# Moving the modulation's products from VectorE to GpSimd and their row sums to ScalarE in a 1-core, two-block transformer kernel

## The reference, cut to what matters

```python
c_act = jax.nn.silu(c)
for i in range(DEPTH_2):                       # 2 layers
    mod = (c_act @ ada_w[i] + ada_b[i])[:, None, :]    # 1024 x 6144 per layer
    sh_a, sc_a, g_a, sh_f, sc_f, g_f = jnp.split(mod, 6, axis=-1)
    h = rms_norm(x, norm_g[i, 0]) * (1.0 + sc_a) + sh_a
    y = attention(h, ...)
    x = x + g_a * rms_norm(y, norm_g[i, 1])
    h = rms_norm(x, norm_g[i, 2]) * (1.0 + sc_f) + sh_f
    x = x + g_f * rms_norm(swiglu_2(h, ffn_w_in[i], ffn_w_out[i]), norm_g[i, 3])
```

## Time and profile before

| | |
|---|---|
| median of 3 runs | 1020.12 us (1019.92 to 1020.59) |
| the profiled execution | 1019.76 us, its span 1018.3 us |
| PE | 992.9 us busy, 98% |
| PEld | 906.0 us, 89% |
| DVE | 687.5 us, 68% |
| ACT | 491.4 us, 48% |
| POOL | 32.1 us, 3% |
| mean DMA rate | 222 GB/s |

### The profile page before, as it was taken

The page is one execution under the profiler, slowest core; times in us unless marked ns, Lnnn a source line. Parts: engine busy times, 40 slices in busy tenths (PEclk is TensorE's granted clock), DMA queues, the critical chain, the costliest instruction groups (busy, mean ns, idle before and its releaser), DMA issues.

```text
span 1018.3 us, 15767 instructions
## 1 busy us (share of the span) xinstructions
PE 992.9 (98%) x6730; PEld 906.0 (89%) x6730; DVE 687.5 (68%) x986; ACT 491.4 (48%) x688; POOL 32.1 (3%) x51
## 2 busy tenths in 40 slices
PE   7999999899999999999999999999999899999997
PEld 6988899779898998899889999997997789999996
DVE  5766756769757767877768768667676766545443
ACT  5644544454334345555564343445667664434341
POOL 2000000010000000100000000001000010000000
PEclk9999999999999999999999999999999999999999
DMA  9653367646887875786467778875643257555511
GB/s 365 260 217 115 125 247 277 220 176 247 317 267 276 297 281 201 274 312 238 177 248 262 299 281 315 302 294 190 202 151 125 83 131 262 173 199 176 198 42 42
DMA packets 33302, 225.64 MB, mean 222 GB/s; under 512 B 3997, under 2 KB 4277, under 8 KB 6864
## 3 DMA queue, kind: packets, MB, share of 16 engines
q1 hardware_dynamic: 31104, 219.00, 59.8%
q0 software_dynamic: 1552, 4.88, 1.4%
q10 hardware_dynamic: 576, 0.74, 0.2%
HBM read 223.54 MB, written 1.08 MB: 221 GB/s over the span
## 4 chain that ended last, share of the span: by engine, by line
PE 88%; DVE 5%; ACT 3%; issue 1%; DMA 1%; POOL 0%; ACTq 0%; DVEq 0%
PE psum L569 18%; PE psum L571 18%; PE psum L570 18%; PE psum L595 8%; PE psum L596 8%; PE psum L597 8%; DVE low L496 2%; PE psum L815 2%; ACT high L490 1%; PE psum L660 1%; PE psum L661 1%; PE psum L662 1%; PE psum L311 1%; PE psum L881 1%; DMA x_res<-in_x 1%
## 5 line engine op out<-in xcount | busy, mean ns | idle before, releaser
L496 DVE TENSOR_TENSOR low<-raw,high 128x2048 fp32r<-128x2048 f32 (+1 forms) x160 | 362.0, 2275 | 162.0 <-ACT high L490 161.5
L569 PE MATMUL psum<-h_hi,high 128*128 128x256 f32 x1504 | 428.9, 285 | 0.0
L570 PE MATMUL psum<-h_lo,high 128*128 128x256 f32 x1504 | 425.5, 283 | 0.0
L571 PE MATMUL psum<-h_hi,low 128*128 128x256 f32 x1504 | 425.5, 283 | 0.0
L490 ACT ACTIVATE high<-raw 128x2048 fp32r<-128x2048 f32 (+1 forms) x160 | 300.8, 1898 | 50.0 <-DMA raw<-in_gate_up 28.9
L569 PEld LDWEIGHTS psum<-h_hi,high 128*128 128x128 f32 x1504 | 288.4, 192 | 4.9 <-issue 2.0
L570 PEld LDWEIGHTS psum<-h_lo,high 128*128 128x128 f32 x1504 | 288.5, 192 | 1.4 <-issue 0.2
L571 PEld LDWEIGHTS psum<-h_hi,low 128*128 128x128 f32 x1504 | 288.5, 192 | 0.0
L595 PE MATMUL psum<-high,y_hi 128*128 128x512 f32 x328 | 129.2, 394 | 2.2 <-DVE y_lo L903 1.7
L596 PE MATMUL psum<-low,y_hi 128*128 128x512 f32 x328 | 128.0, 390 | 0.0
L597 PE MATMUL psum<-high,y_lo 128*128 128x512 f32 x328 | 127.7, 389 | 0.0
(11 more groups left out here) (173 smaller groups left out, 848.2 us busy)
## 6 DMA issues: line engine op xcount, KB each, us to landing
raw<-in_gate_up SPq DMA_DIRECT2D x66, 1024.0 KB, 5.2
raw<-in_ada SPq DMA_DIRECT2D x48, 1024.0 KB, 5.7
raw<-in_down SPq DMA_DIRECT2D x33, 1024.0 KB, 5.2
raw<-in_mix SPq DMA_DIRECT2D x14, 1024.0 KB, 5.1
raw<-in_moba_qk SPq DMA_DIRECT2D x8, 1024.0 KB, 6.9
raw<-in_diff_qk SPq DMA_DIRECT2D x8, 1024.0 KB, 6.4
raw<-in_qk SPq DMA_DIRECT2D x4, 1024.0 KB, 15.8
raw<-in_branch SPq DMA_DIRECT2D x4, 1024.0 KB, 6.0
```

The lines of the kernel that those rows point to most:

```text
L496: nc.vector.tensor_tensor(low[i % N_RAW][:, s], raw[i % N_RAW][:, s], high[n % N_HI][:, s].bitcast(F32), ALU.subtract).then_inc(*rest.up(key))
L569: nc.tensor.matmul(to, a, hi(k), start=first, stop=False)
L570: nc.tensor.matmul(to, a, lo(k), start=False, stop=False)
L571: m = nc.tensor.matmul(to, r, hi(k), start=False, stop=last and j > j0)
```

## The change

The work of `dve_sum` is divided over three engines. GpSimd multiplies the two rows of an ada block by `c_row`, in place (`pool_weigh`, two instructions each, signal `weighed`); calls of it for runs of blocks stand between the other work in GpSimd's program. ScalarE sums each row by a Copy with an accumulator (`act_sum`), in its own order after the rounding of the first slab that stands three or more pieces later in the stream, and signals `summed`. VectorE only calls `dve_modulation` for a finished section, four or more pieces later.

```diff
+        POOL_AT = {m: i for i, (kind, m) in enumerate(STREAM) if kind == "ada"}
+
+        def pool_weigh(*blocks):
+            for m in blocks:
+                i = POOL_AT[m]
+                yield from pool.wait_ge(raw_in[i % N_RAW], i)
+                yield from pool.wait_ge(small_act, "c")
+                for a in range(2):
+                    w = raw[i % N_RAW][:, a * D:(a + 1) * D]
+                    nc.gpsimd.tensor_tensor(w, w, c_row[:, :], ALU.mult).then_inc(*weighed.up((m, a)))
...
-        def dve_sum(i, m):
-            raw_rows = raw[i % N_RAW][:, :].rearrange("p (a n) -> p a n", a=2)
-            yield from dve.wait_ge(raw_in[i % N_RAW], i)
-            yield from dve.wait_ge(small_act, "c")
+        def act_sum(i, m):
             for a in range(2):
-                w = raw_rows[:, a, :]
-                last = nc.vector.tensor_tensor_reduce(
-                    out=w, in0=w, in1=c_row[:, :], scale=1.0, scalar=0.0, op0=ALU.mult, op1=ALU.add,
-                    accum_out=mod_raw[:, 2 * m + a:2 * m + a + 1])
+                w = raw[i % N_RAW][:, a * D:(a + 1) * D]
+                yield from act.wait_ge(weighed, (m, a))
+                last = nc.scalar.activation(w, w, ACT.Copy, accum_out=mod_raw[:, 2 * m + a:2 * m + a + 1])
...
         def act_split(n):
             for i, kind, m in act.items(n):
-                if kind == "main":
-                    yield from act_round(i, m)
+                if kind == "ada":
+                    act_sums.append((i, m))
+                    continue
+                yield from act_round(i, m)
+                while act_sums and act_sums[0][0] + 3 <= i:
+                    yield from act_sum(*act_sums.pop(0))
 
         def dve_split(n):
             for i, kind, m in dve.items(n):
-                if kind == "main":
-                    yield from dve_rest(i, m)
-                else:
-                    yield from dve_sum(i, m)
+                if kind == "ada":
+                    dve_sums.append((i, m))
+                    continue
+                yield from dve_rest(i, m)
+                while dve_sums and dve_sums[0][0] + 4 <= i:
+                    yield from dve_section(dve_sums.pop(0)[1])
...
+            yield from pool_weigh(*range(8))
             yield from pool_post_norm(0)
             yield from pool_table()
+            yield from pool_weigh(*range(8, 12))
             yield from pool_spread()
+            yield from pool_weigh(*range(12, 16))
             yield from pool_gain(0, 0, None)
+            yield from pool_weigh(*range(16, 24))
             yield from pool_post_norm(1)
             yield from pool_gain(0, 1, 0)
+            yield from pool_weigh(*range(24, 32))
             yield from pool_post_norm(2)
+            yield from pool_weigh(*range(32, 48))
             yield from pool_post_norm(3)
```

More of the change, by code:

```diff
@@ L225, in build_program @@
         stored = sig("stored")
+        summed = sig("summed")
         rounded, squared, affined, evacuated, hi_made, exped, probs_copied, small_act = (sig(n) for n in (
             "rounded", "squared", "affined", "evacuated", "hi_made", "exped", "probs_copied", "small_act"))
-        rest, summed, modulated, joined, scaled, h_hi_made, h_lo_made, gained, x_made, produced, lo_made = (sig(n) for n in (
-            "rest", "summed", "modulated", "joined", "scaled", "h_hi_made", "h_lo_made", "gained", "x_made", "produced", "lo_made"))
+        rest, modulated, joined, scaled, h_hi_made, h_lo_made, gained, x_made, produced, lo_made = (sig(n) for n in (
+            "rest", "modulated", "joined", "scaled", "h_hi_made", "h_lo_made", "gained", "x_made", "produced", "lo_made"))
         squared_dve = sig("squared_dve")
@@ L236, in build_program @@
             "slab", "turned", "scored", "applied", "gathered", "small_pe"))
-        scaled_pool = sig("scaled_pool")
+        scaled_pool, weighed = sig("scaled_pool"), sig("weighed")
         powed, small_pool = sig("powed"), sig("small_pool")
@@ L459, in dve_modulation @@
             nc.vector.scalar_tensor_tensor(out=o, in0=o, scalar=2.0 - what, in1=b, op0=ALU.add, op1=ALU.add).then_inc(
-                *summed.up(("biased", key)))
-            yield from dve.wait_ge(summed, ("biased", key))
+                *small_dve.up(("biased", key)))
+            yield from dve.wait_ge(small_dve, ("biased", key))
             g = MOD_GAIN[key]
@@ L508, in dve_sum, with dve_section @@
             section, at = divmod(m, KC // 2)
-            if at < KC // 2 - 1:
-                last.then_inc(*summed.up(m))
-                return
             key = section // 6, section % 6 // 3, section % 3
-            last.then_inc(*summed.up(m, ("section", key)))
-            yield from dve_modulation(*key)
+            last.then_inc(*summed.up(m, *((("section", key),) if at == KC // 2 - 1 else ())))
+        def dve_section(m):
+            section, at = divmod(m, KC // 2)
+            if at == KC // 2 - 1:
+                yield from dve_modulation(section // 6, section % 6 // 3, section % 3)
@@ L516, in act_split @@
+        act_sums, dve_sums = [], []
         def act_split(n):
             for i, kind, m in act.items(n):
-                if kind == "main":
-                    yield from act_round(i, m)
+                if kind == "ada":
[4 more added lines that the diff above has]
+                    yield from act_sum(*act_sums.pop(0))
         def dve_split(n):
             for i, kind, m in dve.items(n):
-                if kind == "main":
-                    yield from dve_rest(i, m)
-                else:
-                    yield from dve_sum(i, m)
+                if kind == "ada":
[4 more added lines that the diff above has]
+                    yield from dve_section(dve_sums.pop(0)[1])
```

## The result

The changed kernel takes **1058.49 us** (median of 4, 1057.44 to 1059.36) where the kernel before took 1020.02 in the same job: ratio 1.0377 [1.0359, 1.0395], slower by 38.5 us. The forecast was 1028.5 with a range to 1040. The profiled execution took 1059.36, with a span of 1058.0 and a mean granted clock of 0.979, 0.997 before.

The account below looks back on a forecast made before the run. PE, busy 992.9 of 1018.3 us, was taken as the bound, so only its waits count. ScalarE's sums at 4.0 plus sharing at 4.4 gave 8.4 us more, 1028.5 us, range 1021.5 to 1040.

Parts of the forecast that it names:

- (a): The merge: ScalarE's sums between roundings make its last part and the norm behind it start 1.0 us later.
- (b): End of the first FFN: block 22's sum delays the third rounding, so VectorE's product PE awaits is 1.15 us later.
- (c): Before the moba norm: block 31's sum between two roundings delays the rest behind them by 1.8 us.
- bounds of 3.0 and 5.3: Low and high ends, in us, for (a) to (c) together, forecast 4.0, from ScalarE's cheapest and dearest row sum.
- rival 2: GpSimd too slow, 4.7 us a product: ScalarE waits, 2 us lost in each of four batches, 1036; chance 0.10.
- (d): Sharing: GpSimd's products delay VectorE's splits after the first and moba norms, 2.2 us each, 4.4 together; low end 0.7.
- Rival 1: Alternating lock at both norms: each VectorE cast and subtraction waits for a product, 8 us a place, 1040; chance 0.17.

Follow-up runs that it names:

- the sums alone: The changed kernel with GpSimd's products left out and ScalarE's row sums kept in place: 1027.21 us, ratio 1.0081.
- the two halves: The changed kernel without GpSimd's products, 1027.21 us, and, separately, with ScalarE's sums shrunk to two columns and products whole, 1048.32 us.
- all remedies: The changed kernel with products held back at four places and row sums of blocks 6, 7, 22, 23, 31 shrunk: 1.0083; repeated, 1027.16 us.

## Why the prediction was wrong

**Right.** A row's sum costs 1.09 us in the forecast, 1.04 in the trace. (a) came out as worked out, 1.0 (0.9 with the sums alone). (b) and (c) had the right places and cause, and shrinking the sums there removed them; they measured 1.4 and 2.0, each 0.2 us more than forecast. (The bounds of 3.0 and 5.3 for the three count one block's sum at the merge, where two stand in the chain; with both they are some 2.6 and 5.7.) For (b) ScalarE's and VectorE's timelines after are, against the earlier trace rows:

```profile
408.23 1.91 ACT L491 ACTIVATE high<-raw 128x2048 fp32r<-128x2048 f32 x1
...
414.05 4.50 DVE L497 TENSOR_TENSOR low<-raw,high 128x2048 fp32r<-128x2048 f32 x2 [1.59 <-ACT high L491]
418.46 0.68 DVE L765 TENSOR_TENSOR work_v<-psum,work_v 128x512 f32<-128x512 f32 x1
```

From the first rounding to VectorE's product it is 10.23 us, 8.86 before, so 1.37 more, which is the whole step: the third rest queues behind the second. A product takes 2.35 us alone and not 2.6, so rival 2 had no ground: ScalarE waits for products 2.3 us in all. (The Trainium skill, GPSIMD Engine Reference, section Performance versus the Vector engine, gives its 4497 ns for an addition, not for a product; half of it, an estimate of 2.3 us, is close to the trace's 2.35 all the same.)

**The step that failed** is (d), in three parts.

1. "If the first cast must wait out a whole product it is 220.1 + 2.6 - 220.5 = 2.2 us. I take the latter". I took one product a place. The queue held four, and all four pass before VectorE's short chain is through: 8.8 and 7.2 us in place of 2.2 each. Letting one block through gave half. Rival 1 had this mechanism and nearly the size, 8 a place, with a chance of 0.17; its turns are right at the moba norm, at the first norm one cast waits for all.

2. "Along the slabs such losses hide (162 us of idle time)." The idle time is an average over all slabs. At the start, at 285, at the flips and at 460 there is none: 9.6 us there. Of these, holding products back removed those at the start and the flips, and more than doubled the one at 285 (4.6 us and not 1.9). I looked for the places where ScalarE's sums meet a short chain, and not for those where VectorE's do.

3. The row I sized sharing by, `h_lo` 0.79 beside GpSimd's instruction, was of another form: TENSOR_SCALAR, one tensor input. With that form 306 us of GpSimd's work stretch L497 by 53 ns; with the product, 279 us stretch it by 357. The Trainium skill's rule of the lock (SBUF — State Buffer, section Who interferes with whom), which I weighed down for this row, was right for the product, which keeps VectorE out to its end. For the one-input form, which also reads SBUF, the traces show the same only for a first part, 0.98 of 2.85 us; the row itself fits that, as GpSimd's instruction began at 13.13, 0.19 us ahead of `h_lo`.

**Not in the sum at all:** the clock, some 8.8 us. With the stretches at half clock that followed at six places, 30.3 us of lost starts cost 39.1. No run holds the clock and changes only the products, so these 8.8 us are counted in the trace and not shown by an experiment.

What stays open: whether the flips are the whole reason why 38.5 us are 3 more than the two halves, which blocks make up the 8 us that remain with all remedies, and what decides between turns and a whole run.

## What to carry to other kernels

Before work goes to GpSimd, count how many of its instructions stand ready at the moment when VectorE has the short chain that TensorE waits for, and price the place at all of them; a wait in GpSimd's queue ahead of such a place gives most of it back. Size contention only from a row of the same form: number of inputs, reads and writes. And ask first whether the work can be moved in time on its own engine: one number in the load order gave 2.4 us where moving it to two other engines cost 38.5.

## What the runs showed of the hardware that I had not expected

- Products queued right behind a GpSimd DMA issue kept VectorE out until the run ended (8.98 and 15.00 us, and 10.67 for two L361 that take 0.88), behind a compute instruction they take turns with it, one each. A 128x4 fill in between didn't change it. Shown by adding DMA issues at one norm, with a control, and by moving them away at the other; the run at 450 is an exception, and why is not shown.
- A fill of GpSimd's (0.956 us) leaves a two-input subtraction at 2290 ns and holds a one-input TENSOR_SCALAR of 0.49 us for a run of four, 4.63 us.
- A one-input GpSimd instruction is slower alone than the two-input product (2.85 against 2.35 us on 1024 columns), and keeps two-input subtractions of VectorE's out for 0.98 us of it, the product for all of its time.
- Copies from PSUM are not held: 0.62 us each beside a product, between instructions of 8 columns held for 2.3.
